# Modulation of the first block by pairs of K-tiles, and gate products between the dot products of a transformer kernel's prelude

## The reference

```python
cond = jax.nn.silu(c)
for l in range(DEPTH):
    mod = jnp.einsum('bd,de->be', cond, w_ada[l]) + b_ada[l]
    sh1, sc1, g1, sh2, sc2, g2, sh3, sc3, g3 = [m[:, None, :] for m in jnp.split(mod, N_MOD, axis=-1)]
    h = modulate(rms_norm(x, norm_ffn1[l]), sh1, sc1)      # h * (1 + scale) + shift
    x = x + 0.5 * g1 * swiglu(h, w_gate1[l], w_up1[l], w_down1[l])
    ...
def swiglu(h, w_gate, w_up, w_down):
    g = jnp.einsum('bsd,df->bsf', h, w_gate)
    u = jnp.einsum('bsd,df->bsf', h, w_up)
    return jnp.einsum('bsf,fd->bsd', jax.nn.silu(g) * u, w_down)
```

## Time and profile before

| | us |
|---|---|
| median of 3 runs | 1189.13 (1187.82 to 1190.16) |
| the profiled execution, its own time | 1189.2 |
| its span, first to last instruction | 1187.5 |
| TensorE busy | 1148.7 (97%) |
| DVE busy | 873.1 (74%) |
| ACT busy | 525.9 (44%) |

### The profile page before, as it was taken

How to read it: one execution, slowest core, us unless ns; L and a number is a source line. 1 busy time by engine, 2 the same in 40 slices (tenths; PEclk the granted TensorE clock), 3 DMA queues, 4 the chain that set the end, 5 groups by cost and what they waited for, 6 DMA issues and landing times.

```text
span 1187.5 us, 20427 instructions
## 1 busy us (share of the span) xinstructions
PE 1148.7 (97%) x7940; PEld 1046.7 (88%) x7940; DVE 873.1 (74%) x1294; ACT 525.9 (44%) x665; POOL 64.6 (5%) x79
## 2 busy tenths in 40 slices
PE   6999999999999999999999999999999998999998
PEld 6889999989898699999978999998989876999996
DVE  7788888778766877766777887888787588645545
ACT  2334334445566533443353344335356555433432
POOL 2011101100000000000001011000000000000000
PEclk9899999989999999999989999999999999999999
DMA  9889998945511667778846988994733244665551
GB/s 305 266 298 304 307 325 304 310 145 178 177 55 54 213 212 249 240 236 264 265 143 213 330 301 296 309 353 152 250 114 101 72 164 159 209 212 188 166 194 72
DMA packets 160369, 258.35 MB, mean 218 GB/s; under 512 B 8366, under 2 KB 127278, under 8 KB 160320
## 3 DMA queue, kind: packets, MB, share of 16 engines
q1 hardware_dynamic: 140739, 182.25, 46.7%
q0 software_dynamic: 19584, 75.50, 19.0%
HBM read 256.56 MB, written 1.05 MB: 217 GB/s over the span
## 4 chain that ended last, share of the span: by engine, by line
PE 75%; DVE 13%; ACT 3%; DMA 3%; DVEq 3%; issue 2%; POOL 0%; ACTq 0%; POOLq 0%
PE bank L1145 15%; PE bank L1146 15%; PE bank L1147 15%; PE bank L1225 7%; PE bank L1221 7%; PE bank L1222 7%; DVE wlo L764 3%; DMA ada<-in_w_ada_dram 3%; DVE room L722 3%; PE bank L1422 2%; PE bank L1163 1%; PE bank L1341 1%; DVE acc L722 1%; ACT whi L438 1%; DVEq L724 1%
## 5 line engine op out<-in xcount | busy, mean ns | idle before, releaser
L438 ACT ACTIVATE whi<-raw 128x2048 fp32r<-128x2048 f32 (+1 forms) x174 | 321.6, 1850 | 25.8 <-DMA raw<-in_w_gate_dram 14.7
L764 DVE TENSOR_TENSOR wlo<-raw,whi 128x2048 fp32r<-128x2048 f32 (+2 forms) x130 | 281.5, 2197 | 22.9 <-ACT whi L438 21.8
L1145 PE MATMUL bank<-hhi,whi 128*128 128x256 f32 (+1 forms) x1008 | 287.7, 285 | 0.0
L1146 PE MATMUL bank<-hlo,whi 128*128 128x256 f32 (+1 forms) x1008 | 285.6, 283 | 0.0
L1147 PE MATMUL bank<-hhi,wlo 128*128 128x256 f32 (+1 forms) x1008 | 285.5, 283 | 0.0
L1145 PEld LDWEIGHTS bank<-hhi,whi 128*128 128x128 f32 (+1 forms) x1008 | 193.1, 192 | 2.4 <-issue 2.0
L1146 PEld LDWEIGHTS bank<-hlo,whi 128*128 128x128 f32 (+1 forms) x1008 | 193.2, 192 | 0.5 <-issue 0.5
L1147 PEld LDWEIGHTS bank<-hhi,wlo 128*128 128x128 f32 (+1 forms) x1008 | 193.1, 192 | 0.0
L481 ACT ACTIVATE eb<-bank 128x512 f32<-128x512 f32 x44 | 26.3, 598 | 362.2 <-PE bank L1225 362.2
L722 DVE SCALAR_TENSOR_TENSOR room<-ada,cT,room 128x512 f32 (+3 forms) x266 | 170.1, 639 | 20.2
L1221 PE MATMUL bank<-hhi,whi 128*128 128x256 f32 x736 | 180.2, 283 | 0.0
(11 more groups left out here) (198 smaller groups left out, 1375.0 us busy)
## 6 DMA issues: line engine op xcount, KB each, us to landing
ada<-in_w_ada_dram POOLq DMA_DIRECT2D x68, 1024.0 KB, 5.8
raw<-in_w_gate_dram SPq DMA_DIRECT2D x44, 1024.0 KB, 6.0
raw<-in_w_up_dram SPq DMA_DIRECT2D x44, 1024.0 KB, 6.8
raw<-in_w_down_dram SPq DMA_DIRECT2D x44, 1024.0 KB, 6.0
raw<-in_w_in_dram SPq DMA_DIRECT2D x28, 1024.0 KB, 5.7
raw<-in_w_out_dram SPq DMA_DIRECT2D x8, 512.0 KB, 3.3
raw<-in_w_out_dram SPq DMA_DIRECT2D x4, 1024.0 KB, 5.7
LG<-in_b_ada_dram SPq DMA_DIRECT2D x6, 512.0 KB, 8.3
```

Of the source, the lines that this page charges most:

```text
L438: last = act.activation(dst, src, ACT.Copy)
L764: last = dve.tensor_tensor(dst, src, hi.bitcast(F32), ALU.subtract)
L1145: pe.matmul(ps, l_hi, r_hi, start=first, stop=False)
L1146: pe.matmul(ps, l_hi, r_lo, start=False, stop=False)
```

## The change

The chunks are loaded in the order 0, 4, 1, 5, 2, 6, 3, 7, so that shift and scale of a pair of K-tiles are complete one pair after the other. Six chunks are dotted (`DOTTED`) and two are weighed (1 and 2). `dot_chunk` is turned round: a column of `cT` is stationary, the chunk is the moving side, and the sum is a row of 256 numbers on one partition; ACT copies it (`copy_row`) and TensorE turns it back into columns (`turn_row`). The transposed x is copied raw to `hTf` by ACT, and DVE modulates it two K-tiles at a time (`first_pair`); high and low parts are made for the pair. GpSimd waits with chunk 6 for the dot product of chunk 0, with chunk 3 for that of chunk 4, and with chunk 7 until chunk 1 is weighed. The first gate load is issued when chunk 0 has landed, the first up load when chunk 6 has. The gate products of the first step are made pair by pair (`gate_pair`, 12 products each) between the other products of the prelude, in two banks; ACT makes silu of that step in two halves, and TensorE's step starts with up. `aliA` and `aliC` are made in steps 0 and 1 of the mixing stage of layer 0. The position tables lie in other buffers than before.

```diff
@@ -149,10 +149,13 @@
...
-        WEIGHED = (1, 3, 5, 7)
-        pre_acc = {1: acc[:, 0:1, :], 3: acc[:, 1:2, :], 5: gate[:, 0:CW].unsqueeze(1), 7: gate[:, CW:2 * CW].unsqueeze(1)}
+        WEIGHED = (1, 2)
+        DOTTED = (0, 4, 5, 6, 3, 7)
+        pre_acc = {1: acc[:, 0:1, :], 2: acc[:, 1:2, :]}
...
@@ -359,8 +371,10 @@
-            sp.wait_ge(ada_full[0], 16)
-            gate_up(0, 0, 0, v_gate, v_up)
+            sp.wait_ge(pre_full[0], 16)
+            fill(0, 0, chunk_cols(raw[0]), v_gate[:, 0:KT, 0:CW])
+            sp.wait_ge(pre_full[6], 16)
+            fill(1, 0, chunk_cols(raw[1]), v_up[:, 0:KT, 0:CW])
...
@@ -404,10 +418,12 @@
-            for m in range(6):
-                pool.dma_start(pre_ada[m][:, 0, :, :], v_ada[:, 0:KT, m * CW:(m + 1) * CW]).then_inc(pre_full[m], 16)
-            for k in range(2):
-                fill(k, 1, slice(0, KT), slice((6 + k) * CW, (7 + k) * CW))
+            for m in (0, 4, 1, 5, 2, 6, 3, 7):
+                if m in (6, 3):
+                    pool.wait_ge(row_done, DOTTED.index(0 if m == 6 else 4) + 1)
+                if m == 7:
+                    pool.wait_ge(pre_used, 1)
+                pool.dma_start(pre_ada[m], v_ada[:, 0:KT, m * CW:(m + 1) * CW]).then_inc(pre_full[m], 16)
...
@@ -595,10 +613,46 @@
+            def copy_row(m):
+                act.wait_ge(row_done, DOTTED.index(m) + 1)
+                if m in (6, 3):
+                    act.sem_inc(ada_used[m % 2], 1)
+                act.activation(pre_row(m), PRE_ROWS[DOTTED.index(m) % 2][0:1, 0:CW], ACT.Copy).then_inc(row_read, 1)
+            def first_high(p):
+                act.wait_ge(first_h, p + 1)
+                act.activation(hhi[:, 2 * p:2 * p + 2, :], hTf[:, 2 * p:2 * p + 2, :], ACT.Copy).then_inc(first_hi, 1)
             act.wait_ge(tables, 1)
             act.preload_act_table_set("natural_log_exp_and_others")
+            act.wait_ge(x_in, 16)
+            for t in range(TT):
+                act.activation(xn[:, t, :], xs[:, t, :], ACT.Square, accum_out=ss[:, t, 0:1])
+                root(t, [D])
+            act.preload_act_table(ACT.Silu)
+            copy_row(0)
+            for t in range(TT):
+                for half in range(2):
+                    act.wait_ge(tp_done, 2 * t + half + 1)
+                    act.activation(hTf[:, 4 * half:4 * half + 4, t * P:(t + 1) * P], TPB[t][half][:, :].rearrange("p (k s) -> p k s", k=4),
+                                   ACT.Copy).then_inc(raw_h, 1)
+            copy_row(4)
+            copy_row(5)
+            first_high(0)
+            first_high(1)
+            split_hi(0, 0)
+            copy_row(6)
+            copy_row(3)
+            first_high(2)
+            copy_row(7)
+            first_high(3)
+            act.sem_inc(hhi_ready, TT)
+            split_hi(1, 0)
             for l in range(L):
-                boundary(l, 0, nth(l, NB * TT, 0))
+                if l > 0:
+                    boundary(l, 0, nth(l, NB * TT, 0))
                 ffn(l, 0, U_IN)
...
@@ -701,16 +756,19 @@
-            for h in range(H_A):
-                dve.scalar_tensor_tensor(aliA[:, h, :], distf, -s_a[h], causal[:, :], ALU.mult, ALU.add)
-            for h in range(H_C):
-                dve.scalar_tensor_tensor(aliC[:, h, :], distf, -s_c[h], maskC, ALU.mult, ALU.add)
+            def alibi(which):
+                if which == 0:
+                    for h in range(H_A):
+                        dve.scalar_tensor_tensor(aliA[:, h, :], distf, -s_a[h], causal[:, :], ALU.mult, ALU.add)
+                else:
+                    for h in range(H_C):
+                        dve.scalar_tensor_tensor(aliC[:, h, :], distf, -s_c[h], maskC, ALU.mult, ALU.add)
-                dve.wait_ge(gains_in, 8 * 16)
...
@@ -726,10 +784,26 @@
-                dve.wait_ge(pre_full[m] if m < 6 else ada_full[m - 6], 16)
-                weigh_rows(pre_acc[m], pre_ada[m])
-                if m in (1, 7):
-                    dve.drain().then_inc(ada_used[1], 1)
+                dve.wait_ge(pre_full[m], 16)
+                weigh_rows(pre_acc[m], pre_ada[m].unsqueeze(1))
+                if m == 1:
+                    dve.drain().then_inc(pre_used, 1)
+            def first_pair(p):
+                ks = slice(2 * p, 2 * p + 2)
+                both = lambda a: a.rearrange("p (m k) -> p m k", m=2)
+                dve.wait_ge(sums_done, p + 1)
+                dve.tensor_tensor(both(modAB[:, :])[:, :, ks], both(PRE_SUMS[p][:, 0:4]), biasL[:, 0:2, ks], ALU.add)
+                dve.drain()
+                dve.scalar_tensor_tensor(modA[:, ks], modA[:, ks], 1.0, colL[:, ks, N_MOD], ALU.add, ALU.mult)
+                dve.drain()
+                dve.wait_ge(raw_h, 2 * TT)
+                for k in (2 * p, 2 * p + 1):
+                    last = dve.tensor_scalar(hTf[:, k, :], hTf[:, k, :], modA[:, k:k + 1], modB[:, k:k + 1], ALU.mult, op1=ALU.add)
+                last.then_inc(first_h, 1)
+                dve.wait_ge(first_hi, p + 1)
+                dve.tensor_tensor(hlo[:, ks, :], hTf[:, ks, :], hhi[:, ks, :].bitcast(F32), ALU.subtract).then_inc(first_lo, 1)
...
@@ -1021,28 +1090,34 @@
+            def layer_columns(l):
+                dve.tensor_copy(colL[:, :, :], cols[:, l, :, :])
+                dve.tensor_copy(biasL[:, :, :], cols[:, l, :, 0:N_MOD].rearrange("p k m -> p m k"))
+                dve.drain()
             dve.wait_ge(silu_c, 1)
-            dve.wait_ge(silu_c, 1)
-            weigh_chunk(1)
-            dve.wait_ge(x_in, 16)
-            dve.sem_inc(x_ready, TT)
-            weigh_chunk(3)
             for t in range(TT):
             late_tables()
-            weigh_chunk(5)
-            weigh_chunk(7)
+            layer_columns(0)
+            weigh_chunk(1)
+            first_pair(0)
+            first_pair(1)
+            split_lo(0, 0)
+            weigh_chunk(2)
+            first_pair(2)
+            first_pair(3)
+            for done in (hTf_ready, h_ready):
+                dve.sem_inc(done, TT)
+            dve.sem_inc(mods_ready, 1)
+            dve.wait_ge(gains_in, 8 * 16)
             for l in range(L):
-                dve.tensor_copy(colL[:, :, :], cols[:, l, :, :])
-                dve.tensor_copy(biasL[:, :, :], cols[:, l, :, 0:N_MOD].rearrange("p k m -> p m k"))
                 dve.tensor_copy(qkgL[:, :], qkg[:, l, :])
-                if l == 0:
-                    dve.wait_ge(modc_done, 1)
-                    modulation(l, 0, PS[3][:, 0:2 * KT])
-                else:
+                if l > 0:
+                    layer_columns(l)
                     modulation(l, 0, modc[:, N_MOD * KT:(N_MOD + 2) * KT])
-                boundary(l, 0, l == 0)
+                    boundary(l, 0)
                 split_lo(1, turn(l, U_FFN[0]))
...
@@ -1050,12 +1125,15 @@
                         head_norm(l, n - 2)
+                    if l == 0 and n in (0, 1):
+                        alibi(n)
                     if n + 2 < NC:
...
@@ -1157,13 +1235,41 @@
-                pe.wait_ge(pre_full[m] if m < 6 else ada_full[m - 6], 16)
+                pe.wait_ge(pre_full[m], 16)
+                n = DOTTED.index(m)
+                if n >= 2:
+                    pe.wait_ge(row_read, n - 1)
+                for k in range(KT):
+                    last = pe.matmul(PRE_ROWS[n % 2][0:1, 0:CW], cT[:, k:k + 1], pre_ada[m][:, k, :], start=k == 0, stop=k == KT - 1)
+                last.then_inc(row_done, 1)
+            def turn_row(m):
+                p = m % 4
+                pe.wait_ge(row_read, DOTTED.index(m) + 1)
                 for j in range(CT):
-                    for k in range(KT):
-                        last = pe.matmul(PS[3][:, m * CT + j:m * CT + j + 1], pre_ada[m][:, 0, k, j * P:(j + 1) * P], cT[:, k:k + 1],
-                                         start=k == 0, stop=k == KT - 1)
-                if m in (0, 6):
-                    last.then_inc(ada_used[0], 1)
+                    at_ = m // 4 * 2 + j
+                    last = pe.matmul(PRE_SUMS[p][:, at_:at_ + 1], pre_row(m)[:, j * P:(j + 1) * P], ones[0:1, 0:1], start=True, stop=True)
+                return last
+            def gate_pair(p):
+                pe.wait_ge(first_hi, p + 1)
+                if p == 0:
+                    pe.wait_ge(split_done[0], 2)
+                wh, wl = chunk_cols(whi[0]), chunk_cols(wlo[0])
+                for low in (False, True):
+                    if low:
+                        pe.wait_ge(first_lo, p + 1)
+                    for ft in range(2):
+                        for k in (2 * p, 2 * p + 1):
+                            ps, cut = (GB, SB_)[ft][:, 0:S], slice(ft * P, (ft + 1) * P)
+                            if low:
+                                last = pe.matmul(ps, wh[:, k, cut], hlo[:, k, :], start=False, stop=k == KT - 1)
+                            else:
+                                pe.matmul(ps, wh[:, k, cut], hhi[:, k, :], start=k == 0, stop=False)
```

(44 more changed lines are left out.)

65 lines of the change are left out of this document (36 added, 29 removed).

## The result

| | before | after |
|---|---|---|
| median of 20 runs each | 1187.83 us (1185.04 to 1198.23) | 1194.39 us (1186.64 to 1198.32) |
| ratio, with its 95% interval | | 1.0047 (1.0033 to 1.0061) |
| the profiled execution | 1189.2 us | 1198.3 us |
| its span | 1187.5 us | 1196.6 us |
| TensorE's mean granted clock, median of the runs | 0.986 (35 runs beside the experiments) | 0.983 |

By the ratio the change makes the kernel slower by 0.47%, 5.6 us; the two medians lie 6.6 us apart. The forecast was 1193.1, slower.

What follows compares the result with a forecast made beforehand. It took DVE's prelude chain, ending with up's split_lo, to set when TensorE may run without stopping. Mark + 2.3, clock + 1.4 and mixing + 0.3 made + 4.0: 1193.1 us, own range 1191.5 to 1196, overall range 1188.0 to 1196.5.

Steps and rivals of the forecast that it cites:

- What bounds: Prelude: DVE's chain sets when TensorE may run without stopping; earlier gate products are worth nothing unless that chain gets shorter.
- the mark: End of up's split_lo in the prelude, 53.77 before, forecast 56.1 (+ 2.3 us); first down product 9.03 us behind it.
- The early gate load: SP's queue: issued at 9.8 instead of 30.22, yet landing no earlier, at 36.1 to 36.6 (36.04 before).
- Rival 1: Gate load gets half of the bytes against the chunks, landing at about 32.2: 1188.7 us, chance 0.18.
- Prelude dot products: TensorE: 3.4 us a chunk at 2.4 GHz, 6.9 at 1.2 GHz; six instead of four, free ahead of the gate weights.
- rival 3: TensorE stays at 1.2 GHz through the prelude dot products, 6.9 us each: + 15, 1204 us, chance 0.06.
- Where the win is lost: Prelude: 8.6 us won at gate's splits, lost through chunk 2's weighing, chunk 7's dot product and up's splits behind pair 3.
- The fall of the clock: Behind the 3.2 us wait for gulo, seven down products at 1.2 GHz, likelier than not: + 1.4 us.
- Rival 2: All as forecast, but no fall of the clock at the wait for gulo: 1191.7 us, chance 0.20.
- The mixing stage: aliA and aliC moved to layer 0's mixing steps, all but 0.3 us hidden: + 0.3, bounds 0 and 1.4.
- The sum: Whole kernel: + 2.3 (mark) + 1.4 (clock) + 0.3 (mixing) = + 4.0 us, to 1193.1, chance 0.47.
- Rival 4: Placement works as meant, DVE's chain shortens by the 5.7 us of gate products, mark at 48: 1184 us, chance 0.09.

Runs made afterwards that it cites:

- run 4: Changed kernel with chunk 2's weighing and chunk 7's dot product ahead of gate's low half and the gate pairs, row 6's copy ahead of gate's high split: 1185.77 us, ratio 0.9963.
- run 5: Changed kernel with the first gate load ahead of the eight head-gain loads in SP's queue: 1190.28 us, ratio 1.0008.
- run 1: Changed kernel with aliA and aliC made in the prelude again instead of mixing steps 0 and 1: 1192.84 us, ratio 1.0028.
- run 2: Changed kernel with 12 products of zeros on TensorE between the first step's up products and first down products: 1191.81 us, ratio 1.0025.
- run 6: Changed kernel with one swap on DVE alone, chunk 2 weighed ahead of gate's low half: 1191.11 us, ratio 0.9997.
- run 7: Changed kernel with the first gate load issued only when chunk 6 has landed: 1193.47 us, ratio 1.0030.
- Run 3: Changed kernel with both splits of the first up weights moved ahead of the last two K-tile pairs: 1187.35 us, ratio 0.9988.
- run 10: Changed kernel with run 5's and run 8's edits, gate's high split ahead of row 6's copy, and later chunk-buffer refills: 1191.27 us, ratio 1.0003.
- run 9: Kernel before the change, with only the position tables moved (other buffers, aliA and aliC in mixing steps 0 and 1): 1190.41 us, ratio 1.0008.
- run 8: Run 4's kernel with up's splits ahead of the last pairs and without the first step's eight zero products: 1187.68 us, ratio 0.9980.
- 4 again: The kernel of run 4 measured a second time, unchanged, beside other experiments: 1184.55 us, ratio 0.9953.

## Why the prediction was right

*What bounds.* Right. The first down product followed the mark by 8.96 us (forecast 9.03) whatever TensorE had done by then: the 24 gate products of pairs 0 and 1, finished by 45.1 instead of behind all modulation, bought nothing. Runs 4 and 5 moved the mark, to 49.24 and 51.39, and the first down product came 8.94 and 8.95 us behind it; in runs 1, 2, 6 and 7 the distance was 8.94 to 8.96. Run 3 took the end of up's `split_lo` off the path, and TensorE's own products set the moment.

*The early gate load.* The landing was forecast at 36.1 to 36.6 and came at 36.05; "no earlier than before" is confirmed by run 7. That the number fits so well is in part luck: the same load landed anywhere from 31.4 to 37.6 in the traces (last section), and the way there was not as told. The prediction had gate begin at 26 and take turns with the chunks to 35. In the trace the chunks' queue did run nearly dry while GpSimd waited with chunk 3 for the dot product of chunk 4 (issued at 23.53), and most of gate's packets went then (packets, MB and share of the 16 engines, 24 to 28.5 us):

```profile
q1 hardware_dynamic: 1114, 0.99, 72.0%
q0 software_dynamic: 151, 0.55, 36.4%
```

I gave that gap up to 1 us. 1 MB had nearly moved by 28.5, yet the load was not complete until 36.05. In between SP's queue moved little at first, 71 packets against 294 of the chunks' from 28.5 to 32, and then 565 against 214, which are mostly of the up load. That fits with one or a few of the 16 engines being behind with gate, but no row shows it.

Whether a queue's turns go by packets or by bytes is seen where both queues are full, in run 10 with the gate load ahead of the gains (12 to 16 us, 4-KB packets of the chunks and 1-KB packets of gate):

```profile
q0 software_dynamic: 286, 1.11, 79.9%
q1 hardware_dynamic: 286, 0.29, 24.4%
```

Equal packets and a quarter of the bytes. The Trainium skill (DMA: Bandwidth & Descriptors, section Queues, rings and completion order) has an engine go round its queues packet by packet, and the counts here agree, with as many of gate's packets to a turn as of the chunks'; how many these are they do not tell. Rival 1, half of the bytes for gate, falls.

*Prelude dot products.* Their price was right (3.4 us forecast, 3.6 measured), and rival 3 fell: the clock was at its upper level from the second chunk on (3.61 us each; the first took 5.28). Dot 4 ended at 23.2, not at my 26. All of it was free, as said.

*Where the win is lost.* Right in place and order (forecast in brackets): gate's splits 36.05 to 40.28 (36.4 to 40.7), chunk 2 weighed to 44.5 (45.0), chunk 7 dotted 45.83 to 49.4 (45.9 to 49.3), modulation of the last pair and its high copy, up's `split_hi` to 54.2 (53.7), mark 56.56 (56.1). The term was + 2.3, and 2.7 was measured at the first down product. One step was incomplete: I put DVE's order on the path and the gate pairs beside it. They were equally long: the trace of run 6 shows that the pairs, at 1.2 GHz behind a wait of 4.7 us (3.96 in the changed kernel), hold the sums of chunk 2 as long as the weighing does.

*The fall of the clock.* Right that it comes, too small in size. I took seven products at 0.2 us, 1.4. In the changed kernel's profile it lasted 6.8 us and not 3.4, which at 0.39 us each is 2.7; run 2 gives 2.6 by its ratio, with wide intervals. Runs 1, 5 and 7 had 3.4 us of it, run 6 none. Rival 2, no fall, is thus not the rule but does happen in single executions.

*The mixing stage.* + 0.3 forecast, no cost in the waits of the changed kernel's trace and in run 9's; run 1, at 1.0028 against 1.0047, leaves room for up to some 2 us that no trace shows.

*The sum.* 2.7 for the mark and 1.4 to 2.7 for the clock make 4.1 to 5.4 of the 5.6 us measured (3.9 to 7.2 by its interval). The granted clocks of the timed runs agree with that: 0.986 to 0.983 is 1190 x 0.003 x 2 = 7 us more at half clock, x 0.39 = 2.8 us, or 2.0 at the 0.28 of the timed executions. So the sum fits the change itself. It does not fit every run: run 5 has its first down product 2.5 us ahead of the one before and a ratio of 1.0008, run 6 has it 3.7 us behind and 0.9997, and that stays open. Rival 4, the placement works as meant, needed the mark at 48. Run 4 reached 46.95 + 2.29 = 49.2 by undoing the placement: there the gate pairs stand behind the dot products again.

## What to carry to other kernels

Filling an engine's idle time with work brings nothing while another chain sets the moment at which it may go on; find that moment (here the end of up's low half) and ask of every moved instruction what it puts behind itself on its own engine. Independent work, such as a weight split whose data is there, must not be queued behind the last step of a dependent chain: moving two instructions ahead of it (run 3) or letting the chain go first (run 4) turned + 0.5% into - 0.1% (no change within its interval) and - 0.4%. But before an in-order engine is given an early wait for a transfer, see how far that transfer's landing spreads: runs 8 and 10 lost their gains to a wait for one.

## What the runs showed of the hardware that was not expected

- The gate load's landing varied from execution to execution, with the same queue order ahead of it: 31.4 us (run 4), 33.8 (3), 34.3 (2), 35.2 (4 again), 35.7 (1), 36.0 (after), 37.0 (6), 37.6 (8). In the changed kernel's trace most of its bytes had moved by 28.5.
- With a 1-MB load ahead of them in the queue, the issues of the small gain loads held SP for 6.53, 4.99, 3.54 and 3.54 us a pair (run 5). With the load behind them, in the changed kernel, a pair took 1.3 to 1.4.
- The granted clock falls in stretches of 3.4 or 6.8 us, and the granted clock of the same program ranged from 0.979 to 0.989 over 20 executions. Over the profiles the time at half clock behind the first down product was 22 to 46 us. Each us of it went with 0.3 to 0.4 us in the changed kernel, so 10 us more or less of it go with 0.25 to 0.35%, as much as most of the edits here; in the kernel before, no such price shows.
